# One rounding and one subtraction per weight slot instead of two halves

## The chip, the cores and the metric
The kernel runs on one core of one Trainium2 chip. The metric is the device time of one launch in microseconds. Everything is float32; matrix products are made of three passes over rounded parts (below).

## What is computed
An encoder trunk of two layers on 256 tokens of width 2048:

```
for l in range(2):
    hn = rms_norm(h, mix_norm_g[l])
    if l == 0: h = h + diff_hgrn_mixer(hn, ...)    # attention heads and a gated recurrence, 8 heads each
    else:      h = h + short_conv_mixer(hn, conv_w_in, conv_w, conv_w_out)
    hn = rms_norm(h, mlp_norm_g[l])
    h = h + square(relu(hn @ w_up)) @ w_down       # 2048 -> 8192 -> 2048
return rms_norm(h, final_norm_g)
```

The short convolution mixer splits `hn @ w_in` into b, c and h, forms `u = c * h`, convolves u with three taps along the tokens and returns `(b * conv) @ w_out`. The weights are 425 MB in all; with 256 tokens every weight is used once.

## The kernel before
**Weights in slots.** The weights pass through the core as 400 slots of 128x2048 numbers (1 MB): four tiles of 128x512. SyncE loads slot `base` into `raw[base % 4]` (`load`, L295). Before it may reuse a place it waits until the low parts of the slot that was there are made (`lo_ready`).

**Split.** A float32 weight becomes a rounded part `w_hi` and the rest, `w_lo = raw - w_hi`, and the product is hi*hi + hi*lo + lo*hi. ACT makes the rounded part (`split_hi`, L314), DVE the rest (`split_lo`, L329). Both work by halves k = 0, 1 of a slot, 128x1024 each. `w_hi` and `w_lo` are rings of `HALVES` = 4 halves, that is of two slots. Three semaphores count halves: `hi_ready`, `lo_ready`, and `w_used`, which PE raises after the last matmul of a half. ACT waits, before half k of slot s+2, until half k of slot s is used.

**Products.** There are two kinds. On an up slot (`multiply_T`, L361) the weights are the stationary side: 48 matmuls with 256 moving columns. On a down slot (`multiply`, L341) the activations are stationary: 24 matmuls with 512 moving columns, into one of the two double banks `pair[0]` and `pair[1]`. PE waits for `lo_ready` of each half.

**Order in an MLP.** `FF_BLOCKS` = 16 blocks of 512 hidden columns. A block has four up slots (into `m23`) and four down slots (`cb` 0 to 3, into `pair[cb % 2]`); the up slots of block i+1 come ahead of the down slots of block i (`both_products`), so that PE sees up, up, up, up, down, down, down, down, and at the layer's end eight down slots in a row. I write u0 to u3 and d0 to d3 for them. After a down slot DVE adds the bank into `h` (`add_scaled`, L1190: two operations, L1195) and raises `pair_read`; PE waits for this before it writes the bank again, which is two down slots later (L844).

**Queues.** Each engine runs its list in program order. In a round p of `both_products`, ACT does what belongs to the activations (`rectify` at p = 4: two relus and two squares, L1072, L1077; `hidden_hi` at p = 1, L1087), and then `split_hi` of the slot two ahead. DVE does `hidden_lo` at p = 2 (L1419), then `split_lo` of the slot two ahead, and at p >= 4 then `add_scaled` of the slot just multiplied (L1427 to L1432):

```
split_lo(dve, at + 4 + p + 2, 8, i)
if p >= 4:
    add_scaled(p - 4, rstd2[:, norm], at + 4 + p, 8, i)
```

**Convolution.** 64 slots: twelve up slots first (c, h, b for block 0), then a loop of two rounds with sixteen slots each (c, h: 8 up slots; four down slots of the output projection, p = 8 to 11; b: four up slots), then a tail that ends in eight down slots. In a round DVE also does `make_u` (L1454, at p = 8, frees `pair[1]`), after which POOL multiplies the same tile (L638), and `convolve` (L1462, at p = 12): twelve small operations ahead of `split_lo` of slot p+2.

**Transitions.** Before each norm's first up slots, PE transposes `h` in four sets (`gain_transpose_pe`, L642), two of them before the last two down slots; ACT and DVE read them out into `xT_hi` and `xT_lo` (L943, L1178).

The slots are numbered through: projections of the mixer 0 to 63, its output 64 to 79, MLP0 from `MLP0_AT` = 80, convolution from 208, MLP1 from 272, `TOTAL` = 400.

Of the kernel before, what the change touches and what calls it, by code (L numbers as in the profile page):

```python
# [27 lines left out]
F32 = mybir.dt.float32  # L28
F32R = mybir.dt.float32r
U32 = mybir.dt.uint32  # L30
ALU = mybir.AluOpType
ACT = mybir.ActivationFunctionType
# [14 lines left out]
HALVES = 4  # L47
# [7 lines left out]
MLP0_AT = OUT_AT + 16  # L55
# [43 lines left out]
def build(nc, x, mix_norm_g, mlp_norm_g, final_norm_g, ab_w_in, ab_w_out, diff_lambda, diff_subln_g,  # L99
          hgrn_lb, hgrn_norm_g, conv_w_in, conv_w, conv_w_out, mlp_w_up, mlp_w_down, out):  # L100
    with ExitStack() as ctx:
        def sb(name, shape, dt=F32):
            return ctx.enter_context(nc.sbuf_tensor(name, shape, dt))
# [4 lines left out]
        def sem(name):  # L108
            return ctx.enter_context(nc.semaphore(name))


        raw = sb("raw", [P, RAW, 4, 512])
        w_hi = sb("w_hi", [P, HALVES, 2, 512], F32R)
        w_lo = sb("w_lo", [P, HALVES, 2, 512], F32R)
# [71 lines left out]
        hi_ready = sem("hi_ready")  # L186
        lo_ready = sem("lo_ready")
        w_used = sem("w_used")
# [93 lines left out]
        def count(scale, const, base, step, i):  # L282

            if isinstance(i, int):
                return scale * (base + step * i) + const
            return i * (scale * step) + (scale * base + const)
# [20 lines left out]
        def landed_at(base, step, i):  # L307


            each, before = (64, 0) if base < MLP0_AT else (16, 48 * (MLP0_AT // RAW))  # L310
            uses = base // RAW + 1
            return i * (each * step // RAW) + (each * uses + before)

        def split_hi(eng, base, step, i, ks=(0, 1)):  # L314
            if base >= TOTAL:
                return
            slot = base % RAW
            if 0 in ks:

                eng.wait_ge(landed[slot], landed_at(base, step, i))  # L320
            for k in ks:
                ring = (2 * base + k) % HALVES
                if 2 * base + k >= HALVES:

                    eng.wait_ge(w_used, count(2, k + 1 - HALVES, base, step, i))
                nc.scalar.activation(w_hi[:, ring], raw[:, slot, 2 * k:2 * k + 2], ACT.Copy  # L326
                                     ).then_inc(hi_ready, 1)

        def split_lo(eng, base, step, i, ks=(0, 1)):  # L329
            if base >= TOTAL:  # L330
                return
            slot = base % RAW
            for k in ks:
                ring = (2 * base + k) % HALVES

                eng.wait_ge(hi_ready, count(2, k + 1, base, step, i))
                nc.vector.tensor_tensor(w_lo[:, ring], raw[:, slot, 2 * k:2 * k + 2],  # L337
                                        w_hi[:, ring].bitcast(F32), ALU.subtract
                                        ).then_inc(lo_ready, 1)
# [593 lines left out]
        def _(eng):  # L933
# [88 lines left out]
            for n in range(2):  # L1022
                split_hi(eng, n, 0, 0)
                if n == 0:
                    norm_hi_of(0, 1)
            for p in range(8):
                if p == 3:
                    eng.wait_ge(rows_T, 2)
                    nc.scalar.activation(gains[:, 32:121], M[3][:, 32:121], ACT.Copy)
                    nc.scalar.activation(lbt[:].rearrange("p a b c -> p (a b c)"),  # L1030
                                         M[3][:, 128:176], ACT.Copy).then_inc(par_act, 1)
                if p == 4:

                    eng.wait_ge(par_dve, 4)
                    nc.scalar.activation(lbt[:], lbt[:], ACT.Exp).then_inc(par_act, 1)
                    nc.scalar.activation(lam_sum[:], lam_sum[:], ACT.Exp).then_inc(par_act, 1)
                if p in (1, 2):
                    norm_hi_of(0, p + 1)
                    squares(0, (2 * p - 2, 2 * p - 1))
                if p == 5:  # L1040
                    eng.wait_ge(rstd_step, 2)
                    copy_product(0, 0)
                split_hi(eng, p + 2, 0, 0)
            with eng.Fori(0, HEADS - 1) as i:
                copy_product(1, i)
                hook(0, i)
                for q in range(16):
                    if q in MIX_AT:
                        hook(MIX_AT[q], i)
                    if q == COPY_AT:  # L1050
                        copy_product(0, i + 1)
                    split_hi(eng, 8 + q // 2 + 2, 8, i, (q % 2,))
                hook(MIX_AT[16], i)
# [117 lines left out]
        def _(dve):  # L1171
# [214 lines left out]
            for n in range(2):  # L1386
                split_lo(dve, n, 0, 0)
                if n == 0:
                    norm_lo_of(0, 1)
            for p in range(8):  # L1390
                if p in (1, 2):
                    norm_lo_of(0, p + 1)
                if p == 3:
                    sum_squares(0)
                    parameters_before_exp()
                if p == 5:
                    parameters_after_exp()
                split_lo(dve, p + 2, 0, 0)
            with dve.Fori(0, HEADS - 1) as i:
                for q in range(16):  # L1400
                    if q in MIX_AT:
                        hook(MIX_AT[q], i)
                    split_lo(dve, 8 + q // 2 + 2, 8, i, (q % 2,))
                hook(MIX_AT[16], i)
# [181 lines left out]
```

## Time and profile before

| | |
|---|---|
| Median of 3 runs | 2364.97 us (2364.95 to 2365.18) |
| Profiled execution, first to last instruction | 2362.9 us |
| PE busy | 2332.4 us, 99% |
| PE weight loads busy | 2108.1 us, 89% |
| DVE busy | 1462.6 us, 62% |
| ACT busy | 1090.2 us, 46% |
| POOL busy | 249.8 us, 11% |
| Data moved | 425.78 MB, 180 GB/s |

The profile is of one execution. Its page gives the span from first to last instruction and no other time of that execution; the runs' median lies 2.1 us above the span. Busy times of the engines lie beside each other and don't add up. PE's matmuls overlap, so their busy time says that PE had work, not that it was at its peak. The mixer of layer 0 takes the first 480 us or so, its output projection ends near 545 us, MLP0 near 1265 us, the convolution near 1630 us, MLP1 near 2350 us.

### The profile page before, as it was taken

The page shows a single profiled execution, that of the slowest core. Times are in us where ns is not written, and L with a number is a line of the kernel's source. Part 1 is how long each engine was busy: PE and PEld are TensorE (multiplying, and loading weights), DVE is VectorE, ACT ScalarE, POOL GpSimd, SP SyncE. Part 2 cuts the span into 40 slices and gives each one's busy share as a digit, 9 for nine tenths or more (in the row PEclk, how much of TensorE's full clock was granted, in tenths as well). Part 3 has the DMA queues.
Part 4 walks back from the last instruction along what each step waited for, and adds up shares of the span by engine and source line. Part 5 has one row for each costly group of instructions (what it writes and reads, how often), then busy time and mean ns, then how long its engine had stood idle before and what let it go on. Part 6 is the DMA issues. An engine that isn't in the chain of part 4 may idle for free.

```text
span 2362.9 us, 38313 instructions
## 1 busy us (share of the span) xinstructions
PE 2332.4 (99%) x14581; PEld 2108.1 (89%) x14581; DVE 1462.6 (62%) x1686; ACT 1090.2 (46%) x1391; POOL 249.8 (11%) x367
## 2 busy tenths in 40 slices
PE   8999999999999999999999999999999999999997
PEld 6888888789899999999989999998998998998996
DVE  5777777755565565565566564656555556555655
ACT  5555554435444444444445334345444444444443
POOL 4445555500000000000000000000000000000000
PEclk9999999999999999999999999999999999999999
DMA  9555555455555555555555555555555555555553
GB/s 257 162 154 157 145 152 166 145 177 170 189 192 181 192 182 194 180 193 182 190 188 176 187 180 183 192 179 178 194 180 194 181 193 182 191 183 189 189 184 125
DMA packets 316175, 425.78 MB, mean 180 GB/s; under 512 B 10537, under 2 KB 141906, under 8 KB 315986
## 3 DMA queue, kind: packets, MB, share of 16 engines
q1 hardware_dynamic: 316066, 424.92, 56.4%
q8 instruction: 43, 0.70, 0.1%
q14 instruction: 18, 0.15, 0.0%
q10 hardware_dynamic: 48, 0.02, 0.0%
HBM read 422.79 MB, written 2.10 MB: 180 GB/s over the span
## 4 chain that ended last, share of the span: by engine, by line
PE 87%; POOL 6%; issue 4%; ACT 1%; DVE 1%; SPq 1%; DMA 0%; POOLq 0%; DVEq 0%; ACTq 0%
PE pair L353 14%; PE pair L355 14%; PE pair L357 14%; PE m L379 11%; PE m L377 11%; PE m L375 11%; PE pair L379 3%; PE pair L375 3%; PE pair L377 3%; POOL lk L577 1%; PE m L726 1%; POOL even L564 1%; POOL kin L577 1%; PE m L790 1%; POOL lk L589 1%
## 5 line engine op out<-in xcount | busy, mean ns | idle before, releaser
L337 DVE TENSOR_TENSOR w_lo<-raw,w_hi 128x1024 fp32r<-128x1024 f32 x800 | 988.8, 1242 | 855.5 <-ACT w_hi L326 854.5
L326 ACT ACTIVATE w_hi<-raw 128x1024 fp32r<-128x1024 f32 x800 | 846.2, 1059 | 1219.3 <-PE pair L357 633.6
L379 PE MATMUL m<-xT_hi,w_lo 128*128 128x256 f32 x2176 | 615.8, 283 | 0.0
L377 PE MATMUL m<-xT_lo,w_hi 128*128 128x256 f32 x2176 | 615.8, 283 | 0.0
L375 PE MATMUL m<-xT_hi,w_hi 128*128 128x256 f32 x2176 | 615.6, 283 | 0.0
L353 PE MATMUL pair<-w_hi,yT_hi 128*128 128x512 f32 x1280 | 499.8, 391 | 1.0 <-DVE h L1208 0.9
L355 PE MATMUL pair<-w_lo,yT_hi 128*128 128x512 f32 x1280 | 498.4, 389 | 0.0
L357 PE MATMUL pair<-w_hi,yT_lo 128*128 128x512 f32 x1280 | 498.1, 389 | 0.0
L375 PEld LDWEIGHTS m<-xT_hi,w_hi 128*128 128x128 f32 x2176 | 417.7, 192 | 1.2
L377 PEld LDWEIGHTS m<-xT_lo,w_hi 128*128 128x128 f32 x2176 | 417.7, 192 | 1.2
L379 PEld LDWEIGHTS m<-xT_hi,w_lo 128*128 128x128 f32 x2176 | 417.7, 192 | 0.0
L353 PEld LDWEIGHTS pair<-w_hi,yT_hi 128*128 128x128 f32 x1280 | 240.4, 188 | 50.8 <-DVE h L1208 1.4
L357 PEld LDWEIGHTS pair<-w_hi,yT_lo 128*128 128x128 f32 x1280 | 240.3, 188 | 50.3
L355 PEld LDWEIGHTS pair<-w_lo,yT_hi 128*128 128x128 f32 x1280 | 240.5, 188 | 48.1
L1195 DVE SCALAR_TENSOR_TENSOR h<-pair,rstd,h 128x512 f32<-128x512 f32 x288 | 202.0, 743 | 5.8 <-PE pair L357 5.8
L353 PE MATMUL pair<-w_hi,xT_hi 128*128 128x512 f32 x512 | 204.1, 399 | 0.0
L357 PE MATMUL pair<-w_hi,xT_lo 128*128 128x512 f32 x512 | 200.0, 391 | 0.0
L355 PE MATMUL pair<-w_lo,xT_hi 128*128 128x512 f32 x512 | 199.7, 390 | 0.0
L375 PE MATMUL pair<-xT_hi,w_hi 128*128 128x256 f32 x640 | 181.6, 284 | 0.0
L379 PE MATMUL pair<-xT_hi,w_lo 128*128 128x256 f32 x640 | 181.1, 283 | 0.0
L377 PE MATMUL pair<-xT_lo,w_hi 128*128 128x256 f32 x640 | 181.1, 283 | 0.0
L516 POOL TENSOR_SCALAR meansq<-meansq 128x2 f32<-128x2 f32 x5 | 1.0, 193 | 1607.4 <-DVE meansq L1188 1607.4
(147 smaller groups left out, 1711.0 us busy)
## 6 DMA issues: line engine op xcount, KB each, us to landing
raw<-in_mlp_w_up SPq DMA_DIRECT2D x128, 1024.0 KB, 5.2
raw<-in_mlp_w_down SPq DMA_DIRECT2D x128, 1024.0 KB, 5.0
raw<-in_ab_w_in SPq DMA_DIRECT2D x256, 256.0 KB, 3.9
raw<-in_conv_w_in SPq DMA_DIRECT2D x48, 1024.0 KB, 5.2
raw<-in_ab_w_out SPq DMA_DIRECT2D x64, 256.0 KB, 4.1
raw<-in_conv_w_out SPq DMA_DIRECT2D x16, 1024.0 KB, 5.0
h<-in_x SPq DMA_DIRECT2D x4, 512.0 KB, 5.9
out_dram<-h SPq DMA_DIRECT2D x8, 256.0 KB, 2.4
```

The lines of the kernel that those rows point to most:

```text
L326: nc.scalar.activation(w_hi[:, ring], raw[:, slot, 2 * k:2 * k + 2], ACT.Copy).then_inc(hi_ready, 1)
L337: nc.vector.tensor_tensor(w_lo[:, ring], raw[:, slot, 2 * k:2 * k + 2], w_hi[:, ring].bitcast(F32), ALU.subtract).then_inc(lo_ready, 1)
L353: nc.tensor.matmul(dst[:, tt], hi[:, kt, cols], w_hi[:, ring, q], start=begin, stop=False)
L355: nc.tensor.matmul(dst[:, tt], hi[:, kt, cols], w_lo[:, ring, q], start=False, stop=False)
L357: mm = nc.tensor.matmul(dst[:, tt], lo[:, kt, cols], w_hi[:, ring, q], start=False, stop=end)
L375: nc.tensor.matmul(dst[:, c], w_hi[:, ring, q, cols], xT_hi[:, kt], start=begin, stop=False)
L377: nc.tensor.matmul(dst[:, c], w_hi[:, ring, q, cols], xT_lo[:, kt], start=False, stop=False)
L379: mm = nc.tensor.matmul(dst[:, c], w_lo[:, ring, q, cols], xT_hi[:, kt], start=False, stop=end and c % 2 == 1)
L564: nc.gpsimd.tensor_tensor(both(even, lv)[:, :, :, 1], first[:, :, 0::2], second[:, :, 0::2], ALU.mult)
L577: mark(nc.gpsimd.tensor_tensor(dst.rearrange("p (a b) -> p a b", b=m), src.rearrange("p (a b) -> p a b", b=m), factor.unsqueeze(2).broadca ...
L589: mark(nc.gpsimd.tensor_copy(dst.rearrange("p (a b c) -> p a b c", b=2, c=m)[:, :, 1], kin[:, 1].rearrange("p (a b c) -> p a b c", b=2, c= ...
L1195: ins = nc.vector.scalar_tensor_tensor(out=h[:, tt, cols], in0=pair[cb % 2][:, tt], scalar=factor[:, tt:tt + 1], in1=h[:, tt, cols], op0=A ...
```

## The change
From slot `MLP0_AT + 2` on, `split_hi` waits until the whole slot two back is used, rounds the whole slot in one ACT operation of 128x2048 and raises `hi_ready` by 2. `split_lo` waits for both counts, subtracts in one DVE operation of 128x2048 and raises `lo_ready` by 2. PE's code stays: it waits by halves, and both counts now come together. The ring has the same four halves, used as two whole slots. The slots before keep the two halves.

```diff
@@ split_hi
                 eng.wait_ge(landed[slot], landed_at(base, step, i))
+            if base >= MLP0_AT + 2:
+                eng.wait_ge(w_used, count(2, 2 - HALVES, base, step, i))
+                ring = 2 * base % HALVES
+                nc.scalar.activation(w_hi[:, ring:ring + 2], raw[:, slot], ACT.Copy
+                                     ).then_inc(hi_ready, 2)
+                return
             for k in ks:
@@ split_lo
             slot = base % RAW
+            if base >= MLP0_AT + 2:
+                ring = 2 * base % HALVES
+                eng.wait_ge(hi_ready, count(2, 2, base, step, i))
+                nc.vector.tensor_tensor(w_lo[:, ring:ring + 2], raw[:, slot],
+                                        w_hi[:, ring:ring + 2].bitcast(F32), ALU.subtract
+                                        ).then_inc(lo_ready, 2)
+                return
             for k in ks:
```

## Rows read from the trace of the kernel before

**Rows 1.** The page: engine, busy us (share of the span), instructions.
```profile
PE 2332.4 (99%) x14581; PEld 2108.1 (89%) x14581; DVE 1462.6 (62%) x1686; ACT 1090.2 (46%) x1391; POOL 249.8 (11%) x367
```

**Rows 2.** Busy time by stretch: length, PE, PEld, DVE, ACT, POOL, clock, DMA.
```profile
580.00:2340.00 1760.00, 1760.00 (x11636) 1626.03 (x11635) 1038.55 (x1066) 782.99 (x884) 12.70 (x10) 1.00 0.57 185
```

**Rows 3.** Timeline of ACT in MLP0: start, us, engine, line, operation [idle before].
```profile
901.98 1.06 ACT L326 ACTIVATE w_hi<-raw 128x1024 fp32r<-128x1024 f32 x1 [1.82 <-PE m L379]
904.86 1.06 ACT L326 ACTIVATE w_hi<-raw 128x1024 fp32r<-128x1024 f32 x1 [1.82 <-PE m L379]
905.83 1.07 ACT L1072 ACTIVATE sm<-m 128x512 f32<-128x512 f32 x2
...
907.82 1.06 ACT L326 ACTIVATE w_hi<-raw 128x1024 fp32r<-128x1024 f32 x1
910.32 1.06 ACT L326 ACTIVATE w_hi<-raw 128x1024 fp32r<-128x1024 f32 x1 [1.45 <-PE pair L357]
```

**Rows 4.** Timeline of DVE on the down slots that follow.
```profile
911.42 1.23 DVE L337 TENSOR_TENSOR w_lo<-raw,w_hi 128x1024 fp32r<-128x1024 f32 x1 [1.29 <-ACT w_hi L326]
912.56 1.40 DVE L1195 SCALAR_TENSOR_TENSOR h<-pair,rstd,h 128x512 f32<-128x512 f32 x2
...
918.00 1.40 DVE L1195 SCALAR_TENSOR_TENSOR h<-pair,rstd,h 128x512 f32<-128x512 f32 x2
```

**Rows 5.** Timeline of PE: the first matmul of the second down slot.
```profile
910.12 0.39 PE L353 MATMUL pair<-w_hi,yT_hi 128*128 128x512 f32 x1
```

**Rows 6.** Groups by line and shape over the span: count, busy us, mean ns, idle.
```profile
L326 ACT ACTIVATE w_hi<-raw 128x1024 fp32r<-128x1024 f32 x800 | 846.2, 1059 | 1219.3 <-PE pair L357 633.6
L1126 ACT ACTIVATE yT_hi<-lq 128x1024 fp32r<-128x1024 f32 x4 | 4.2, 1043 | 0.0
L1087 ACT ACTIVATE yT_hi<-sm 128x512 fp32r<-128x512 f32 x64 | 36.4, 616 | 0.0
L337 DVE TENSOR_TENSOR w_lo<-raw,w_hi 128x1024 fp32r<-128x1024 f32 x800 | 988.8, 1242 | 855.5 <-ACT w_hi L326 854.5
L1496 DVE TENSOR_TENSOR yT_lo<-lq,yT_hi 128x1024 fp32r<-128x1024 f32 x4 | 4.9, 1219 | 0.0
L1419 DVE TENSOR_TENSOR yT_lo<-sm,yT_hi 128x512 fp32r<-128x512 f32 x64 | 41.2, 684 | 0.0
```

**Rows 7.** Timeline of DVE, ACT and PE where PE waits for a bank (output projection).
```profile
496.33 1.28 DVE L1208 TENSOR_TENSOR h<-pair,h 128x512 f32<-128x512 f32 x2
496.75 1.06 ACT L326 ACTIVATE w_hi<-raw 128x1024 fp32r<-128x1024 f32 x1 [1.60 <-PE pair L357]
...
498.00 0.40 PE L355 MATMUL pair<-w_lo,yT_hi 128*128 128x512 f32 x1
```

**Rows 8.** Timeline of DVE and POOL around `make_u` in the convolution's loop.
```profile
1383.33 1.22 DVE L1459 TENSOR_TENSOR proj_a<-pair,proj_a 128x1024 f32<-128x1024 f32 x1
...
1384.62 2.40 POOL L638 TENSOR_TENSOR proj_a<-proj_a,bias 128x1024 f32<-128x1024 f32 x1 [66.66 <-DVE proj_a L1459]
...
1384.93 4.30 DVE L337 TENSOR_TENSOR w_lo<-raw,w_hi 128x1024 fp32r<-128x1024 f32 x2 [0.39 <-ACT w_hi L326]
```

**Rows 9.** Timeline of ACT and DVE around `convolve` in the same loop.
```profile
1402.88 1.06 ACT L326 ACTIVATE w_hi<-raw 128x1024 fp32r<-128x1024 f32 x1 [1.66 <-PE pair L357]
...
1406.43 1.13 DVE L1472 TENSOR_SCALAR lq<-proj_a,gains 128x256 f32<-128x256 f32 x4
...
1411.12 3.48 DVE L337 TENSOR_TENSOR w_lo<-raw,w_hi 128x1024 fp32r<-128x1024 f32 x3
```

**Rows 10.** Timeline of PE and DVE at MLP0's end: transposes, and their reading.
```profile
1251.07 1.03 PE L657 MATMUL m<-ident,h 128*128 128x128 f32 x8
...
1254.82 1.65 DVE L1178 SCALAR_TENSOR_TENSOR xT_lo<-m,gains,xT_hi 128x256 fp32r<-128x256 f32 x4
```

**Rows 11.** DMA issues: tile, queue, count, KB each, median us to landing.
```profile
raw<-in_mlp_w_up SPq DMA_DIRECT2D x128, 1024.0 KB, 5.2
```

## The prediction
> **What bounds the kernel now.** I read the busy times first: PE is busy for 99% of the span, DVE for 62% [rows 1]. The stages then say where: between 580 and 2340 us PE is busy 1760.00 of 1760.00 us at full granted clock [rows 2]. From the first MLP on, PE's own pace is the time. A change on ACT and DVE can gain nothing there; it can only open gaps in PE. So the question is how late the last thing is that PE needs at the start of each slot, and how much room it has.
>
> The pace: ACT's releases lie 2.88 us apart on an up slot [rows 3], so such a slot takes 5.76 us. One down slot's addition into `h` starts 5.44 us after the last [rows 4], so a down slot takes 5.44 us. I call E(s) the moment at which PE has done slot s and, unhindered, takes up s+1. PE's first matmul of the second down slot is at 910.12 and ACT starts the half released by it at 910.32 [rows 3, 5]: 0.20 us from E to ACT.
>
> **Part 1: the operations.** Each slot from MLP0_AT+2 on loses two ACT and two DVE operations of 128x1024 and gets one each of 128x2048. No row has that size, so I extrapolate from the same engine and kind at 512 and 1024. ACT: 616 and 1043 ns, 0.834 ns an element; 1059 + 1024 x 0.834 = 1.91 us. DVE: 684 and 1219 ns, 1.045 ns an element; 1.23 + 1.07 = 2.30 us [rows 4, 6]. Bounds: 1.88 (0.80 ns an element, a little under any pair of rows) and 2.12 us (two halves, nothing saved) for ACT, 2.25 and 2.46 us for DVE; I take the extrapolation, which is nearest to like operations. The saved fixed parts, some 0.2 us of each engine a slot, fall into idle time, since ACT and DVE wait for PE and not PE for them: worth nothing. POOL's and PE's instructions stay the same.
>
> **Part 2: the waits.** Before, each half went through ACT and DVE as soon as the same half of the slot two back was used. So the first half was done in the shade of the second, and only the second stood behind E(s). Now the whole slot s+2 stands behind E(s): ACT from E+0.20 to E+2.11, DVE from E+2.15 (0.04 us from ACT's end to DVE's start, 910.32+1.06 against 911.42) to E+4.45 [rows 3, 4]. PE needs it at E(s+1), which is E(s) + 5.44 or + 5.76. For PE's resumption after DVE's end there is one stall to read: DVE ends at 496.33+1.28 = 497.61, and PE's second matmul is at 498.00, at a pace of 5.44/24 = 0.23, so PE is back as if it had started at 497.77: 0.16 us [rows 7]. The weights are ready at E+4.61, inside even the shorter slot, by 0.83 us. No up slot stalls for its weights alone. Where ACT has more to do first, it has room: the rectifying (905.83 to 907.82, some 2 us [rows 3]) now follows the whole-slot rounding and ends at E + 0.20 + 1.91 + 2.0 = E+4.1, before the next release at E+5.64.
>
> **Part 3: what is queued behind.** DVE's order on a down slot is: the low part of s+2, then `add_scaled` of slot s. Both wait for E(s). The next DVE operation starts 1.14 us after a 1.23 us one began (911.42, 912.56), so 0.09 before its end, and the addition takes 1.40 [rows 4]. Before, the second half's addition was done at 0.20+1.10+1.14+1.40 = E+3.84. Now it is 0.20+1.91+0.04+(2.30-0.09)+1.40 = E+5.76, and PE can go at E+5.92. Down slot s+2 writes the same `pair` bank and waits for that addition; it wants to start at E+5.44. Stall: 0.48 us.
> How often: in a group of four, d2 waits for d0's addition. PE then starts d2 0.48 late, but d1 ended on time, and d3's chain runs from E(d1): E(d1)+5.92 is just when the late d2 ends. So d3 pays nothing more. It is one stall for two consecutive down slots. That ACT is released while PE stands still is in the one stall to read: ACT starts at 496.75, PE only after 497.61 [rows 7]. d0 and d1 of a group follow four up slots and find their banks free. In each MLP groups 0 to 13 give one stall each, and the last two, eight down slots on end, give three: 17 a layer, 34 in both, 34 x 0.48 = 16.3 us.
>
> **Part 4: the convolution.** In the loop (two rounds) `make_u` takes the place of an addition before down slot 1, 1.22 us instead of 1.40 [rows 8]: 5.74 - 5.44 = 0.30. Then POOL's 2.40 us operation [rows 8] reaches some 0.45 us into DVE's next low part; the row says a DVE operation beside it took over 3 us, so they exclude each other. Down slot 2 may start at E + 5.44 + 5.92 + 0.45 = 11.81 and, after the first 0.30, wants to at 11.18: 0.63. In the same round `convolve` stands between d3's addition and the low part of slot p+2 = 14: from E of d3, low part at 2.15, addition at 4.36, `convolve` at 5.68, and 4.69 us later (1406.43 to 1411.12 [rows 9]) the low part at 10.37; ready at 12.83. PE wants it two up slots on, at 11.52: 1.31 us. Before, E was 1402.68 and the same queue moved on at 1411.12, 8.44 behind E, so it made it with the two halves. A round loses 0.30+0.63+1.31 = 2.24, both 4.5. The tail has six down slots that find a bank busy, two by two (the first of them waits for its weights behind `convolve`): three times 0.48, 1.4.
>
> **Part 5: the transitions.** Before the last two down slots PE does transposes of 1.03 us, and DVE 1.65 us of `xT_lo` after them [rows 10], which now starts only behind a later addition. PE's second set of transposes waits for the bank that this reads: some 0.3 us late at MLP0's end and 0.6 at the convolution's, 0.9 together. The sets inside the next stage have slots of 5.76 + 0.8 us and fit.
> Loads: a raw slot is free 1.9 us later, after 4.45 instead of 2.53 us; a load lands in 5.2 us [rows 11] and has three slots, over 16 us. Hidden; at twice the landing time it still would be.
>
> **Sum:** 16.3 + 4.5 + 1.4 + 0.9 = 23.1 us. On the profiled execution's span of 2362.9 that is 2386.0; the median of the runs lies 2.1 us above that span, and 2365.0 + 23.1 = 2388.
>
> A rule on this. What the rows show first: PE has no gap, and DVE and ACT are busy for 1039 and 783 of 1760 us [rows 2]. The Trainium skill, Perfetto Trace Analysis, section Optimizing Scalar/DVE Operations, says that larger operations can improve throughput if the engine is saturated, and that where these engines are not saturated but cause bubbles elsewhere, breaking instructions up may let work finish sooner. By its first half the change saves time, by its second it costs; the row puts this kernel under the second. By the first half alone the sum would be nothing.
>
> **Rivals.**
> (a) Nothing is saved by the larger size: 2.12 and 2.46 us. The chain is 6.29, the stall 0.85; 34 x 0.85 = 28.9, the rounds 3.4 each, the tail 2.6, transitions 1.5: 40 us, 2405. For it: nothing but the missing row; against it, the pairs at 512 and 1024 in rows 6.
> (b) Every down slot with a busy bank pays its own 0.48, because the release of d1 comes late as well: 68 stalls instead of 34: 32.6, the tail 2.9, rounds and transitions 5.4, together 41 us, 2406. Against it: ACT's start in the middle of the one stall.
> (c) Not slower: the chain fits into the down slot. It decides at 5.44 us; it would take a rounding and a subtraction that last 3.73 us together instead of 4.21, by a faster rate per element in long operations. `convolve` would still cost 1.31 - 0.48 = 0.83 a round, 1.7 us: 2367, within what counts as no change. For it: DVE and ACT have idle time; against it: both rates are the same in all rows. The Trainium skill (VectorE: DVE Perf Modes, The perf-mode tier table) has 2293 ns for an fp32 tensor_tensor of 2048 elements, always in the 1x mode; by that the chain stays at 5.9.
> (d) The change doesn't do what it says (the operation is taken apart again, the waits stay by halves): no change, 2365.
>
> **Chances.** Forecast 0.82, (a) 0.07, (b) 0.06, (c) 0.03, (d) 0.02. The range: the lower end takes the short bounds (1.88, 2.25) and a resumption of 0.10 us instead of 0.16; with about 43 stalls in all (34 + 6 + 3) that is 43 x 0.14 = 6 us less, 2382, and 2381 as end. The upper end lets the extrapolation be short by half of its distance to (a), 2397, and goes on to 2402 for a share of (a) and (b). A measurement of this kernel can't tell less than about 0.2%, 4.7 us, from no change. Faster 0.02, same 0.04, slower 0.94.
>
> **What would show it.** ACT at 1.91 and DVE at 2.30 us for 128x2048; PE idle about 0.5 us at each third down slot, released by DVE's L1195 addition, and none at the fourth; none at up slots but the one behind `convolve`, where DVE's `w_lo` is the releaser; in all some 25 us of PE idle that is new, and the granted clock at 1.00 as before. It would be wrong if PE's gaps stood at every down slot, if they were put down to `w_lo` in the up slots, or if the two operations together took under 3.8 us.

## The result and the profile after

The changed kernel takes 2397.82 us (median of 4 runs, 2397.20 to 2399.29), the kernel before 2364.98: a ratio of 1.0139, 95% interval [1.0125, 1.0154]. It is 32.8 us slower; 23 us were forecast, 2388, range 2381 to 2402. Direction and place of the stalls were right, and in the MLPs their number too. Their size was 0.7 us and not 0.48.

The page of the changed kernel (columns as in [rows 1]), the same stretch as [rows 2], and the new operations by line and shape:

```profile
PE 2348.3 (98%) x14581; PEld 2104.5 (88%) x14581; DVE 1407.5 (59%) x1368; ACT 1029.3 (43%) x1073; POOL 249.7 (10%) x367
```
```profile
580.00:2340.00 1760.00, 1743.71 (x11510) 1597.05 (x11509) 963.43 (x737) 709.46 (x560) 12.75 (x10) 1.00 0.56 183
```
```profile
L342 DVE TENSOR_TENSOR w_lo<-raw,w_hi 128x2048 fp32r<-128x2048 f32 x318 | 729.7, 2295 | 826.2 <-ACT w_hi L324 826.2
L324 ACT ACTIVATE w_hi<-raw 128x2048 fp32r<-128x2048 f32 x318 | 609.2, 1916 | 1082.0 <-PE m L392 490.3
```

Over the span DVE and ACT have 55 and 61 us less to do. PE, which had no gap in this stretch, has gaps of 16.29 us in all. The two durations are 1.92 and 2.295 us, against 1.91 and 2.30 worked out from [rows 6]. The clock stays at 1.00. Who made PE wait from the first MLP on (engine, line waited for: us, times, longest):

```profile
PE pair L366 <- DVE h L1208: 13.2, 33, 0.4
PE m L388 <- DVE w_lo L342: 2.3, 2, 1.2
PE pair L366 <- issue: 0.8, 2, 0.4
PE pair L366 <- DVE proj_a L1472: 0.4, 2, 0.2
PE m L670 <- DVE h L1208: 0.3, 1, 0.3
```

The additions (L1208, before L1195) hold the banks, `convolve`'s queue holds the weights twice, `make_u` holds its bank twice, as parts 3 and 4 had it. I also counted in the records each place where one matmul starts over 0.45 us after the last: none before, 43 after, with 24.0 us beyond PE's pace. Of the 43, 34 lie in the MLPs and 6 in the convolution's rounds. In the convolution's tail the count depends on where the line is drawn: five down slots on end each begin with a step of 0.36 to 0.50 us, and two of these are over 0.45; the third one counted there stands before a transpose.

The forecast had some 25 us of new PE idle; the waits above sum to 17, though 32 us are lost. A matmul's record lasts 0.39 us at a pace of 0.23, so a step of 0.80 us shows as 0.42 us of idle time, and the slower matmuls after a gap (below) show as none.

One group of four down slots of MLP0, ACT, DVE and then PE (compare [rows 3 to 5]):

```profile
917.40 1.92 ACT L324 ACTIVATE w_hi<-raw 128x2048 fp32r<-128x2048 f32 x1 [1.54 <-PE pair L370]
922.84 1.92 ACT L324 ACTIVATE w_hi<-raw 128x2048 fp32r<-128x2048 f32 x1 [3.52 <-PE pair L370]
928.98 1.92 ACT L324 ACTIVATE w_hi<-raw 128x2048 fp32r<-128x2048 f32 x1 [4.22 <-PE pair L370]
```
```profile
919.42 2.29 DVE L342 TENSOR_TENSOR w_lo<-raw,w_hi 128x2048 fp32r<-128x2048 f32 x1 [3.17 <-ACT w_hi L324]
921.63 1.40 DVE L1208 SCALAR_TENSOR_TENSOR h<-pair,rstd,h 128x512 f32<-128x512 f32 x2
924.86 2.29 DVE L342 TENSOR_TENSOR w_lo<-raw,w_hi 128x2048 fp32r<-128x2048 f32 x1 [1.83 <-ACT w_hi L324]
927.07 1.40 DVE L1208 SCALAR_TENSOR_TENSOR h<-pair,rstd,h 128x512 f32<-128x512 f32 x2
```
```profile
922.36 0.39 PE L370 MATMUL pair<-w_hi,yT_lo 128*128 128x512 f32 x1
...
923.16 0.49 PE L366 MATMUL pair<-w_hi,yT_hi 128*128 128x512 f32 x1 [0.42 <-DVE h L1208]
...
923.50 0.40 PE L368 MATMUL pair<-w_lo,yT_hi 128*128 128x512 f32 x1
```

d2's first matmul was due 0.23 us after 922.36 and comes at 923.16, 0.13 us after DVE's addition ends (921.63+1.40). ACT's starts show the rhythm: 5.44, then 6.14 us. The block of eight slots takes 45.53 us instead of 44.82 (in both layers' loops 45.53 to 45.58): 0.71 us more, one stall a group.

By stages, between PE's first transposes ahead of each norm: MLP0 732.54 us instead of 720.64 (+11.9, 17 stalls), the convolution 374.79 instead of 367.33 (+7.5), from there to the end 756.98 instead of 744.50 (+12.5). Together 31.8. The 2.0 us that the profiled execution shows beyond this lie ahead of the first changed slot; the first transposes come at 529.3 to 532.4 us in the kernels of this study, whose code is the same up to there.

### The profile page after: what moved, and what is told of

It is laid out like the page before. It is cut to its first block, busy times and chain, and to the rows that moved or that the text cites. A ratio compares the mean times of both kernels' runs of the same rounds, so it can differ in the third digit from the quotient of the medians.

```text
span 2396.7 us, 37753 instructions
## 1 busy us (share of the span) xinstructions
PE 2348.3 (98%) x14581; PEld 2104.5 (88%) x14581; DVE 1407.5 (59%) x1368; ACT 1029.3 (43%) x1073; POOL 249.7 (10%) x367
## 4 chain that ended last, share of the span: by engine, by line
PE 78%; issue 7%; POOL 5%; DVE 4%; ACT 4%; SPq 1%; DMA 0%; POOLq 0%; DVEq 0%; ACTq 0%
PE pair L366 12%; PE pair L370 11%; PE pair L368 11%; PE m L388 11%; PE m L392 11%; PE m L390 11%; PE pair L388 3%; PE pair L392 3%; PE pair L390 3%; ACT w_hi L324 3%; DVE h L1208 2%; PE m L739 1%; POOL lk L590 1%; DVE w_lo L342 1%; POOL even L577 1%
## 5 line engine op out<-in xcount | busy, mean ns | idle before, releaser
L342 DVE TENSOR_TENSOR w_lo<-raw,w_hi 128x2048 fp32r<-128x2048 f32 x318 | 729.7, 2295 | 826.2 <-ACT w_hi L324 826.2
L324 ACT ACTIVATE w_hi<-raw 128x2048 fp32r<-128x2048 f32 x318 | 609.2, 1916 | 1082.0 <-PE m L392 490.3
L366 PE MATMUL pair<-w_hi,yT_hi 128*128 128x512 f32 x1280 | 505.9, 395 | 15.6 <-DVE h L1208 13.2
L350 DVE TENSOR_TENSOR w_lo<-raw,w_hi 128x1024 fp32r<-128x1024 f32 x164 | 203.1, 1262 | 119.3 <-ACT w_hi L332 119.0
L332 ACT ACTIVATE w_hi<-raw 128x1024 fp32r<-128x1024 f32 x164 | 172.3, 1058 | 232.2 <-PE pair L370 225.6
L1208 DVE SCALAR_TENSOR_TENSOR h<-pair,rstd,h 128x512 f32<-128x512 f32 x288 | 202.1, 744 | 4.4 <-PE pair L370 4.4
```

What stands on the lines that cost most here:

```text
L324: nc.scalar.activation(w_hi[:, ring:ring + 2], raw[:, slot], ACT.Copy).then_inc(hi_ready, 2)
L342: nc.vector.tensor_tensor(w_lo[:, ring:ring + 2], raw[:, slot], w_hi[:, ring:ring + 2].bitcast(F32), ALU.subtract).then_inc(lo_ready, 2)
L366: nc.tensor.matmul(dst[:, tt], hi[:, kt, cols], w_hi[:, ring, q], start=begin, stop=False)
L1208: ins = nc.vector.scalar_tensor_tensor(out=h[:, tt, cols], in0=pair[cb % 2][:, tt], scalar=factor[:, tt:tt + 1], in1=h[:, tt, cols], op0=A ...
```

## The experiments

Ratios are to the kernel before, measured beside each kernel on the same chip; its medians were 2365.02 us (e1 to e4), 2365.17 (e5 to e8) and 2364.95 (e9). I write Q for the theory of the prediction: the bank's release is queued behind a whole slot's low part.

**e1: the addition first.**

```diff
-                        split_lo(dve, at + 4 + p + 2, 8, i)
                         if p >= 4:
                             add_scaled(p - 4, rstd2[:, norm], at + 4 + p, 8, i)
+                        split_lo(dve, at + 4 + p + 2, 8, i)
```
(and so in the four other places where an addition follows a low part)

> The changed kernel, but on every down slot (both MLPs, the convolution's output) DVE does the addition into h before the low part of slot s+2 and not behind it. Theory Q (the time is lost in the queue: the bank's release stands behind a low part of 2.29 us): the addition is done 1.7 us after E, the bank waits go, the weights are ready 4.7 us after E as in the changed kernel, inside 5.44. What stays is make_u behind a low part (two gaps of 0.4 us), and at most 0.5 us at convolve: 2365.5 to 2369 us. Rival W (the weights themselves come too late for PE once a slot is rounded whole): nothing changes, 2390 to 2400, and PE's gaps are put down to w_lo.

Measured: 2366.34 us, ratio 1.0006 [0.9997, 1.0015]. DVE on the down slots, and PE's waits from the first MLP on:

```profile
911.02 1.41 DVE L1208 SCALAR_TENSOR_TENSOR h<-pair,rstd,h 128x512 f32<-128x512 f32 x2 [1.10 <-PE pair L370]
913.10 2.29 DVE L342 TENSOR_TENSOR w_lo<-raw,w_hi 128x2048 fp32r<-128x2048 f32 x1 [0.67 <-ACT w_hi L324]
916.46 1.41 DVE L1208 SCALAR_TENSOR_TENSOR h<-pair,rstd,h 128x512 f32<-128x512 f32 x2 [1.07 <-PE pair L370]
```
```profile
PE pair L366 <- DVE proj_a L1472: 0.4, 2, 0.2
```

The same operations, the same waits for the ring, and 31.5 of the 32.8 us are gone by an order on one engine. The addition fits into DVE's idle time before the rounding is done: the low part starts 0.67 us after it. What is left are chiefly `make_u`'s two gaps. Rival W falls: whole slots are not late for PE.

**e2 and e3: one engine whole, the other in halves.** Each removes the new branch from `split_hi` (e2) or from `split_lo` (e3).

```diff
 def split_hi(...):                          # e2; e3: the same in split_lo
-            if base >= MLP0_AT + 2:
-                ...
-                return
```

> The changed kernel with ACT back at two halves, each waiting for its own half of the ring; DVE stays at one operation of 128x2048. Theory Q: ACT's second half ends 1.26 us after E, DVE's low part starts at 1.36, the addition at 3.57 and ends at 4.97, PE could go at 5.2, before 5.44: no bank wait. convolve leaves about 0.5 us a round. 2365.5 to 2368 us. Rival D (it is DVE's long operation that holds up the addition, whatever ACT does): as the changed kernel, 2395 to 2399.

> The changed kernel with DVE back at two halves, ACT stays at one operation of 128x2048 that raises the count by two. Theory Q: two DVE halves take 2 x 1.14 where the long one takes 2.21 up to the addition, and start 0.07 earlier, their wait being in the instruction: the chain to the bank is the same to 0.05 us, and the bank waits stay at 0.7 us each. Behind convolve PE needs only the first half, 1.07 us earlier, twice: 2394 to 2398 us. Rival D: 2365 to 2370.

Measured: e2 2365.94 us, 1.0005 [0.9996, 1.0014]; e3 2395.25 us, 1.013 [1.0114, 1.0145]. DVE in e2, then in e3:

```profile
911.81 2.29 DVE L336 TENSOR_TENSOR w_lo<-raw,w_hi 128x2048 fp32r<-128x2048 f32 x1 [3.17 <-ACT w_hi L326]
914.02 1.40 DVE L1202 SCALAR_TENSOR_TENSOR h<-pair,rstd,h 128x512 f32<-128x512 f32 x2
```
```profile
917.94 2.36 DVE L343 TENSOR_TENSOR w_lo<-raw,w_hi 128x1024 fp32r<-128x1024 f32 x2 [3.11 <-ACT w_hi L324]
920.22 1.40 DVE L1201 SCALAR_TENSOR_TENSOR h<-pair,rstd,h 128x512 f32<-128x512 f32 x2
```

The long DVE operation costs nothing: from its start to the addition's it is 2.21 us, the two halves take 2.28. What costs is ACT's whole slot. It does away with the overlap in which DVE made the first half's rest while ACT rounded the second half. e2 undoes two things at once on ACT, the long operation and the late start of the first half; e7 below takes the late start alone. ACT in halves, each started as early as before, is enough; e2 has only two short gaps behind `convolve` left. Rival D falls on both.

**e7: the wait without the long operations.**

```diff
 for k in ks:                                # split_hi of the kernel before
-    eng.wait_ge(w_used, count(2, k + 1 - HALVES, base, step, i))
+    late = 2 if base >= MLP0_AT + 2 else k + 1
+    eng.wait_ge(w_used, count(2, late - HALVES, base, step, i))
```

> The kernel before, with two halves on both engines, but from slot MLP0_AT+2 on both halves wait until the whole slot two back is used. This is the change's wait without its long operations. Theory Q: the halves overlap from ACT to DVE, so the addition is done at 0.20+1.10+1.14+1.14+1.40 = 4.98 us after E and PE could go at 5.2, before 5.44: no gap, 2364.5 to 2366.5 us. Rival (the ring's wait for the whole slot is what costs): gaps as in the changed kernel, over 2385.

Measured: 2365.29 us, 0.9998 [0.9989, 1.0008]; PE has no gap:

```profile
580.00:2340.00 1760.00, 1760.00 (x11636) 1625.58 (x11636) 1006.21 (x1066) 752.61 (x883) 12.72 (x10) 1.00 0.56 186
```

So part 2's waits alone cost nothing. ACT and DVE in e7:

```profile
916.18 2.01 ACT L327 ACTIVATE w_hi<-raw 128x1024 fp32r<-128x1024 f32 x2 [3.43 <-PE pair L358]
```
```profile
917.28 2.36 DVE L338 TENSOR_TENSOR w_lo<-raw,w_hi 128x1024 fp32r<-128x1024 f32 x2 [1.76 <-ACT w_hi L327]
919.55 1.40 DVE L1196 SCALAR_TENSOR_TENSOR h<-pair,rstd,h 128x512 f32<-128x512 f32 x2
```

DVE starts 1.10 us after ACT and not behind both roundings: that overlap is what keeps the chain short. With the late start, it takes one whole operation on ACT to lose it, as e3 shows. One combination was not run: ACT late and in halves, DVE whole. My estimate from these rows is 0.20+2.01+0.10+2.21+1.40+0.25 = 6.2 us, as long as the changed kernel's 6.14, so the larger DVE operation is free only where ACT's first half starts early (e2) or the addition goes first (e1).

**e4: the counts raised by 1.** This is about the size. In the changed kernel the hops are longer than in [rows 3, 4]: PE to ACT 0.26 us instead of 0.20, ACT to DVE 0.10 instead of 0.03 (medians over the records). In its records, ahead of each long operation, there is an instruction that only waits; before, the wait stood in the operation itself. What differs in form is the raise by 2.

```diff
-                                     ).then_inc(hi_ready, 2)
+                                     ).then_inc(hi_ready, 1)
-                eng.wait_ge(hi_ready, count(2, 2, base, step, i))
+                eng.wait_ge(hi_ready, count(1, WHOLE + 1, base, step, i))    # WHOLE = MLP0_AT + 2
-                                        ).then_inc(lo_ready, 2)
+                                        ).then_inc(lo_ready, 1)
```
(and the waits of PE and SyncE recounted; PE waits once a slot)

> The changed kernel with both counts raised by 1 for a whole slot and all waits recounted; operations and their order stay. In the profile of the changed kernel a raise by 2 has its wait as an instruction of its own ahead of the operation, and the hops from PE to ACT and from ACT to DVE are 0.26 and 0.10 us instead of 0.20 and 0.03. Theory I (the raise by 2 costs these 0.13 us in every chain): the operations start 0.20 and 0.03 us after their releasers, each of the 43 gaps is 0.13 us shorter, 5.5 us less: 2391 to 2393.5 us. Rival L (the hops grow with the length of the operation): 2396.5 to 2399, hops as in the changed kernel.

Measured: 2391.74 us, 1.0114 [1.0098, 1.0129], 6.1 us less than the changed kernel. ACT, DVE and PE on the same slots:

```profile
920.70 1.92 ACT L328 ACTIVATE w_hi<-raw 128x2048 fp32r<-128x2048 f32 x1 [3.52 <-PE pair L377]
```
```profile
917.21 2.29 DVE L346 TENSOR_TENSOR w_lo<-raw,w_hi 128x2048 fp32r<-128x2048 f32 x1 [3.17 <-ACT w_hi L328]
...
922.65 2.29 DVE L346 TENSOR_TENSOR w_lo<-raw,w_hi 128x2048 fp32r<-128x2048 f32 x1 [1.83 <-ACT w_hi L328]
```
```profile
920.28 0.39 PE L377 MATMUL pair<-w_hi,yT_lo 128*128 128x512 f32 x1
920.95 0.49 PE L373 MATMUL pair<-w_hi,yT_hi 128*128 128x512 f32 x1 [0.29 <-DVE h L1218]
```

ACT starts at 920.70, 0.19 us after d2 was due (920.28+0.23); DVE at 922.65, 0.03 after ACT's end. The step over the gap is 0.67 us instead of 0.80. The hop goes with how the count is raised, not with the length of the operation: theory I, and L falls.

**e5 and e8: the bank's wait last.** PE resumed 0.130 us after the addition inside the loops and 0.054 outside, where [rows 7] was read. e5 is the changed kernel with the edit below; e8 adds e4's.

```diff
 def down(cb, base, step, i, n):             # PE, both MLPs
+                    pe.wait_ge(lo_ready, count(2, 1, base, step, i))
                     pe.wait_ge(pair_read[cb % 2], n * 2 + (before + cb // 2))
-                    multiply(...)
+                    multiply(..., ready=True)      # no wait for lo_ready at k = 0
```

> The changed kernel, but PE on an MLP's down slot waits first for the low part and then for the bank. In the profile of the changed kernel the bank's wait inside the loops stands in a register instruction ahead of the wait for the low part, and PE starts 0.130 us after DVE's end; at the gaps outside the loops, 0.054. Theory H (this order costs 0.075 us at each of the 26 MLP gaps in the loops): all hops are 0.055, steps over the gap 0.73 instead of 0.81 us, 2.0 us less: 2395 to 2397 us. Rival: the hop is that of the longer addition or of the loop as such; the steps stay at 0.81 and the time at 2397 to 2399.

> The changed kernel with both counts raised by 1 for a whole slot and, on an MLP's down slots, the bank's wait last. This leaves the chain that the prediction reckoned with, hops of 0.20, 0.03 and 0.05 us. If those three hops were all that was mis-sized, the MLP gaps are 0.5 us and the time is 2388.5 to 2390.5 us (forecast 2388). If the two don't add up, 2391 to 2392.

Measured: e5 2397.62 us, 1.0135 [1.0119, 1.0151]; e8 2391.78, 1.0113 [1.0097, 1.0129]. The hop did fall to 0.054 and the step over the gap from 0.807 to 0.733 us in all loops. But the time did not move, and a block still takes 45.53 us. My expectation for e5 missed, and e8 came out at its second value: the two hops don't add up. PE's steps in e5's group, d2 and then d3:

```profile
922.74 0.50 PE L367 MATMUL pair<-w_hi,yT_hi 128*128 128x512 f32 x1 [0.34 <-DVE h L1211]
...
928.09 0.39 PE L371 MATMUL pair<-w_hi,yT_lo 128*128 128x512 f32 x1
928.31 0.43 PE L367 MATMUL pair<-w_hi,yT_hi 128*128 128x512 f32 x1
928.58 0.39 PE L369 MATMUL pair<-w_lo,yT_hi 128*128 128x512 f32 x1
```

In this group d3's second matmul comes 0.27 us after the first, not 0.23, and the slot takes 5.52 us instead of 5.46: PE loses at d3 most of what it had won at d2. My reading is that d3's bank stands on the chain from E(d1), which did not move when d2 got away sooner. The records don't show this: d3's first matmul is not late, and in 11 of the 26 loop groups d3 takes at most 0.01 us more than in the changed kernel and it is d2's own slot that takes 0.02 to 0.06 us more. On average over the groups d2 starts 0.075 us sooner, its slot takes 0.023 us more and d3's 0.029 more, so 0.02 us a block is left. Why the rest is lost stays open. Outside the loops the new order made the hop longer, 0.146 us; e8's block is 45.39 us against e4's 45.41.

**e6 and e9: everything mended.** e4 with e1, and:

```diff
-                    if p == 8:
+                    if p == 7:                                  # e9: p == 8 again
                         make_u(i + 1, CONV_AT + 19, 16, i)
-                    if p == 12:
-                        convolve(i + 1)
+                    if p >= 12 and p < 15:
+                        convolve(i + 1, (p - 12,))              # one of its three passes
```

> The changed kernel's whole-slot operations with counts raised by 1, DVE's additions ahead of the low part, make_u one round earlier and convolve spread over three rounds. Every gap that was found has its cause taken away. Theory Q: PE is without a gap from the first MLP on and the time is that of before, 2364 to 2366.5 us; no faster, since PE's own pace is the bound. Rival T (fewer operations on ACT and DVE are worth something once the queues are right): under 2362.5.

> The kernel of e6_all_mended with make_u back in its old round (p = 8), behind a low part; all else as there. In e6 three gaps of 0.73, 0.73 and 0.35 us were left, each behind a low part of 3.84 to 3.99 us that ran beside POOL's 2.39 us operation, which make_u had released earlier. Theory P (DVE's low part and POOL's operation exclude each other, and the earlier make_u brought them together in front of PE): these three go, two gaps of about 0.24 us at make_u's bank come back, PE's gaps from the first MLP on sum to under 0.6 us instead of 1.7, the time is 0.8 to 1.5 us under e6's, 2365 to 2366.5. Rival: the long low parts come from the spread convolve, and the gaps stay.

Measured: e6 2366.97 us, 1.0008 [0.9999, 1.0017]; e9 2365.33 us, 1.0003 [0.9994, 1.0012]. e6 had three gaps where I expected none, and its time lies 0.5 us above the expected range. DVE, POOL and PE in e6:

```profile
1381.85 1.23 DVE L1482 TENSOR_TENSOR proj_a<-pair,proj_a 128x1024 f32<-128x1024 f32 x1 [1.62 <-PE pair L402]
1383.71 3.99 DVE L346 TENSOR_TENSOR w_lo<-raw,w_hi 128x2048 fp32r<-128x2048 f32 x1 [0.63 <-ACT w_hi L328]
```
```profile
1383.16 2.39 POOL L661 TENSOR_TENSOR proj_a<-proj_a,bias 128x1024 f32<-128x1024 f32 x1 [62.54 <-DVE proj_a L1482]
```
```profile
1387.76 0.50 PE L373 MATMUL pair<-w_hi,yT_hi 128*128 128x512 f32 x1 [0.57 <-DVE w_lo L346]
```

With `make_u` earlier, POOL's operation runs from 1383.16 to 1385.55, and DVE's low part, begun at 1383.71, takes 3.99 us instead of 2.29: 1.70 us more for 1.84 us beside it. In e9 the three gaps are gone and two of 0.24 us at `make_u`'s bank are back; this, and not the two times, whose intervals overlap, tells e9 from e6. PE is busy for

```profile
580.00:2340.00 1760.00, 1759.84 (x11636) 1625.30 (x11635) 996.49 (x754) 722.92 (x571) 12.74 (x10) 1.00 0.56 186
```

with whole slots on both engines, 42 us less work on DVE and 60 on ACT than in [rows 2]. It is as fast as before and not faster: no version beats the kernel before, because PE's pace is the bound in all that are free of gaps.

## Why the prediction was right, and what it missed

**Bound (right).** No gap before, so only gaps could change the time; e7 and e9 show the floor. Rivals (c) and (d) are out: the operations are whole, last 4.21 us together, and PE stalls.

**Part 1 (right).** 1.916 and 2.295 us. The saved fixed parts were worth nothing, as e9 shows with both operations whole. Rival (a) is out.

**Part 2 (right in what it says of the weights).** No up slot waits but behind `convolve`. The hops in it were too short, below.

**Part 3 (mechanism right, size wrong).** One stall for two consecutive down slots: in MLP0's loops each group has one long gap, and 43 long gaps in all, as counted. Rival (b) is out; e1 shows that the queue is the cause. The stall was 0.71 us or a little more in a block against 0.48. Its terms, predicted and measured: PE to ACT 0.20, 0.26; ACT 1.91, 1.92; ACT to DVE 0.04, 0.10; low part to addition 2.21, 2.21; addition 1.40, 1.40; resumption 0.16, 0.25 (0.13 to the first matmul, the rest in slower ones after it: the second comes 0.33 us after the first instead of 0.23). That is 6.14 instead of 5.92 us, a stall of 0.70. Of the 0.22 that I missed, e4 shows 0.12 to 0.13 to be the raise by 2, which the diff shows and whose form in [rows 3, 4] I did not compare. The rest is at PE. Its hop inside a loop was read at a place outside the loops, but e5 shows that shortening this hop alone gains next to nothing. "d3 pays nothing more" holds to about 0.02 us in the changed kernel (5.456 us for d3 against 5.44), and less well once d2 starts sooner. How much of the remaining 0.09 us is the slower matmuls after a gap and how much the two chains' coming so close was not separated.

**Part 4 (near in its sums, not in its single terms).** The step before slot 14 was 1.43 us, 1.31 beyond the pace, as forecast; the next matmul adds 0.10, which was not in it. DVE and PE there:

```profile
1423.89 1.13 DVE L1485 TENSOR_SCALAR lq<-proj_a,gains 128x256 f32<-128x256 f32 x4
...
1428.57 2.28 DVE L342 TENSOR_TENSOR w_lo<-raw,w_hi 128x2048 fp32r<-128x2048 f32 x1
```
```profile
1430.91 0.39 PE L388 MATMUL m<-xT_hi,w_hi 128*128 128x256 f32 x1 [1.15 <-DVE w_lo L342]
```

I set each matmul's start in the changed kernel beside the same matmul's start before. In the first round the slot behind `make_u` loses 0.49 us (forecast 0.30), the next one 0.52 (0.63), a third one, which was to pay nothing, 0.20, and the place behind `convolve` 1.40 (1.31). Each round loses 2.63 us instead of 2.24. The term for POOL was too large:

```profile
1400.87 2.41 POOL L651 TENSOR_TENSOR proj_a<-proj_a,bias 128x1024 f32<-128x1024 f32 x1 [66.61 <-DVE proj_a L1472]
```
```profile
1402.83 2.59 DVE L342 TENSOR_TENSOR w_lo<-raw,w_hi 128x2048 fp32r<-128x2048 f32 x1 [2.04 <-ACT w_hi L324]
```

They do share 0.45 us, as forecast, but DVE's low part lasts 0.30 us longer (2.59 instead of 2.29) and not 0.45. So it is partly luck that the second slot comes near its forecast: this term was too large and the hops were too short. In the tail the loss is not "two by two": five down slots on end lose 0.28 to 0.39 us each, and with the transition the tail loses 2.5 us instead of 1.4 + 0.6. So the 43 stalls that the prediction adds up and the 43 that I counted agree by luck in the tail's three.

**Part 5 (near).** PE's second set of transposes loses 0.23 us at MLP0's end (forecast 0.3) and 0.50 at the convolution's (0.6). No wait of PE is put down to a load. Parts 4 and 5 with MLP0's last group came to about 6 us for the convolution's stage; it was 7.5.

**The sum.** 34 MLP stalls at 0.70 instead of 0.48 are 7.5 us of the 8.7 that lie between 23.1 and the 31.8 of the stages. The 1 us left to the 32.8 of the medians is within what the part before the first changed slot varies by.

**The rule.** The Trainium skill, Perfetto Trace Analysis, section Optimizing Scalar/DVE Operations, weighs larger operations for a saturated engine against smaller ones where an unsaturated engine causes bubbles on another. This case agrees with its second half: e2 gives 2365.94 us with the rounding in halves, against 2397.82. But e1 has 2366.34 us with nothing broken up, by the order on DVE alone.

## What to carry to other kernels

Where two engines work one behind the other for a third, cutting the work into pieces is what lets them overlap; count the chain from the release of the buffer to the last thing that is queued behind it, not only to the operation itself. Here the merge was free on the second engine (e2) and cost everything on the first (e3), as long as the order of the queue stayed. And before merging, look at what stands in the queue behind the long operation: moving a short operation that is already due ahead of it gave back all but 1.3 us here (e1 against the kernel before on the same chip).

## What the runs showed of the hardware

A raise of a semaphore by 2 instead of 1 made the wait an instruction of its own and cost 0.06 to 0.07 us in each hop (0.26 and 0.10 against 0.20 and 0.03 us; e4 turns both back). After PE has stood still, its next matmuls of 512 columns come at 0.33 and then 0.231 to 0.236 us instead of 0.227; so a gap costs about 0.1 us beyond its length. In e5 a group whose d3 had its second matmul 0.04 us late took 0.06 us more for that slot. On DVE, a subtraction that began beside POOL's multiplication lost the time that they shared less some 0.15 us: 1.70 of 1.84 us in e6, 0.30 of 0.45 in the changed kernel, and by [rows 8] 1.94 of 2.09 for two halves (4.30 us instead of the 2.36 of e7).
